# One transformer step on one core: FFN gate and up projections of ten blocks by Strassen's seven quarter products, hidden values through DRAM, down projection with the inner tiles outermost

## The reference, cut to what matters

```
h2 = _rmsnorm(x, norm2_g) * (1 + scale2) + shift2
a, b = jnp.split(h2 @ w_gu, 2, axis=-1)        # 1024 x 5632: gate half, up half
x = x + gate2 * ((jax.nn.silu(a) * b) @ w_down)   # 2816 x 1024
```

## Time and profile before

| what | us |
|---|---|
| median of 3 runs | 2062.1 (2058.85 to 2065.07) |
| the profiled execution, its time | 2066.32 |
| its span, first to last instruction | 2064.4 |
| PE busy | 1999.6 (97%) |
| DVE, ACT, POOL busy | 941.5, 609.5, 559.3 |

### The profile page before, as it was taken

The page is one execution under the profiler, slowest core; times in us unless marked ns, Lnnn a source line. Parts: engine busy times, 40 slices in busy tenths (PEclk is TensorE's granted clock), DMA queues, the critical chain, the costliest instruction groups (busy, mean ns, idle before and its releaser), DMA issues.

```text
span 2064.4 us, 26414 instructions
## 1 busy us (share of the span) xinstructions
PE 1999.6 (97%) x10768; PEld 1756.4 (85%) x10768; DVE 941.5 (46%) x1712; ACT 609.5 (30%) x1093; POOL 559.3 (27%) x392
## 2 busy tenths in 40 slices
PE   8999898899999999899999999999999999999998
PEld 3899788798889889788888888888888888888887
DVE  5699954255566665337416651312303213123035
ACT  3512222355455555344313211111111111111113
POOL 0000000434344442134432332232222222322225
PEclk9899999999999999999999999999999999999999
DMA  8552333733333441556520321111111111111112
GB/s 306 184 159 62 113 120 105 166 100 85 94 94 93 105 102 58 166 162 193 183 73 21 92 62 41 42 41 41 32 41 41 41 31 42 41 33 40 41 41 102
DMA packets 198807, 185.19 MB, mean 90 GB/s; under 512 B 33696, under 2 KB 174240, under 8 KB 197664
## 3 DMA queue, kind: packets, MB, share of 16 engines
q1 hardware_dynamic: 198688, 183.52, 29.7%
HBM read 142.60 MB, written 40.89 MB: 89 GB/s over the span
## 4 chain that ended last, share of the span: by engine, by line
PE 54%; DVE 2%; DMA 1%; issue 0%; ACT 0%; POOL 0%; SPq 0%; DVEq 0%; ACTq 0%
PE ps_all L144 53%; DMA branch_and_gates<-branch_dram 1%; DVE normed L2021 1%; DVE AL L2027 1%; DVE normed L2015 1%; DMA gates<-last_gates 0%; PE ps_all L1685 0%; DVE y L2063 0%; POOL w_lo L1904 0%; PE ps_all L1619 0%; PE ps_all L1618 0%; PE ps_all L1672 0%; DVE XT L1992 0%; PE ps_all L1643 0%; ACT w_hi L1762 0%
## 5 line engine op out<-in xcount | busy, mean ns | idle before, releaser
L144 PE MATMUL ps_all<-AH,w_hi 128*128 128x512 f32 (+3 forms) x2112 | 767.8, 364 | 31.7 <-PEq L229 7.4
L144 PE MATMUL ps_all<-AL,w_hi 128*128 128x512 f32 (+3 forms) x2112 | 756.2, 358 | 0.0
L144 PE MATMUL ps_all<-AH,w_lo 128*128 128x512 f32 (+3 forms) x2112 | 755.7, 358 | 0.0
L144 PEld LDWEIGHTS ps_all<-AH,w_hi 128*128 128x128 f32 x2112 | 403.8, 191 | 74.7 <-issue 23.2
L144 PEld LDWEIGHTS ps_all<-AH,w_lo 128*128 128x128 f32 x2112 | 402.8, 191 | 42.0
L144 PEld LDWEIGHTS ps_all<-AL,w_hi 128*128 128x128 f32 x2112 | 404.4, 191 | 39.1
L1904 POOL TENSOR_TENSOR w_lo<-w_raw,w_hi 128x1024 fp32r<-128x1024 f32 x78 | 194.6, 2494 | 555.7 <-ACT w_hi L1762 555.7
L1992 DVE SCALAR_TENSOR_TENSOR XT<-ps_all,mod,XT 128x512 f32<-128x512 f32 (+1 forms) x288 | 187.3, 662 | 204.3 <-PE ps_all L144 194.3
L2043 DVE TENSOR_TENSOR hidden<-ps_all,silu_a 128x512 f32<-128x512 f32 (+1 forms) x66 | 39.8, 602 | 504.1 <-PE ps_all L144 504.1
L144 PE MATMUL ps_all<-actH,w_hi 128*128 128x512 f32 (+1 forms) x528 | 188.7, 357 | 0.0
L144 PE MATMUL ps_all<-actL,w_hi 128*128 128x512 f32 (+1 forms) x528 | 188.3, 357 | 0.0
(11 more groups left out here) (172 smaller groups left out, 2538.2 us busy)
## 6 DMA issues: line engine op xcount, KB each, us to landing
w_raw<-w_gu_dram SPq DMA_DIRECT2D x44, 512.0 KB
w_raw<-w_in_dram SPq DMA_DIRECT2D x42, 512.0 KB
wmod_then_mixers<-w_mod_dram SPq DMA_DIRECT2D x20, 1024.0 KB, 8.8
branch_and_gates<-gates SPq DMA_DIRECT2D x16, 768.0 KB, 4.4
w_raw<-w_down_dram SPq DMA_DIRECT2D x22, 512.0 KB
gates<-gate_rows SPq DMA_DIRECT2D x42, 224.0 KB, 1.9
kq_src<-kT_dram SPq DMA_DIRECT2D x16, 384.0 KB, 6.0
xT_dram<-xT_then_mixers SPq DMA_DIRECT2D x1, 5120.0 KB, 17.3
```

The lines of the kernel that those rows point to most:

```text
L144: mm = nc.tensor.matmul(out, w, a[:, k, cols[0]:cols[1]], start=(first and part == 0), stop=(last and part == 2))
```

## The change

The first block (hidden tiles 0 and 1) is computed as before. For the other ten, each side (gate, up) of a block is one "pair" p, 20 in all: its 1024 x 256 weights are seen as 2 x 2 quarters (input half, hidden tile), the latent rows as 2 x 2 quarters (input half, chunk), and the product is made by Winograd's form of Strassen's method, with seven quarter products P1 to P7 of 4 input tiles x 3 matmuls x 512 columns instead of eight. The context chunk stays classic (X0, X1: 24 matmuls of 256 columns each).

- Row sums: `t_sums` makes four sums of row quarters once, 16 DVE instructions; ACT and DVE split them (`T_hi`, `T_lo`; one of them over the columns of chunk 1 in AH and AL).
- Weight sums: for each pair a 1 MB load (`load_pair`), 4 DVE instructions (`weight_sums`), and 8 slots of 128 x 512 (4 quarters, 4 sums), each split by ACT (`upper_slot`) and POOL (`lower_slot`). Ten slots form a ring.
- Results: for each pair ACT copies P1 and DVE makes 7 additions with one operand in PSUM (`add`); after the up side DVE multiplies the five quarters with the silu of the gate side (`hidden_quarter`).
- The hidden values go to DRAM by chunk and tile and come back in the down projection. That runs after all pairs, as 66 groups n = (chunk c, hidden tile k) with the chunk outermost: in each group 8 output tiles x 3 matmuls into 8 PSUM banks, summed over all k in PSUM (`down_group`). Each group loads a 512 KB row block of `w_down` (three raw buffers, four split ones) and its hidden chunk, so `w_down` is loaded and split three times.
- The residual rows are written back to DRAM before the normalisation, which now works in place, and are loaded again during the down projection; the output is added once, at the end of each chunk (`last_residual`).
- The final sums of squares and the transposes of chunks 0 and 1 run between the down groups of chunk 2. Four matmuls with zeros open the banks that two 256-column sums share.
- gate2 is made in 8 parts beside the first 8 pairs. After the first and the second phase POOL clears 59 and 31 semaphores.

```diff
...
+def clear(g):
+
+    for signal in g.used:
+        g.nc.gpsimd.sem_clear(signal)
...
+def product_order():
+
+    order = [(0, "P1")]
+    for p in range(PAIRS_FFN):
+        order += [(p, name) for name in (("P2", "P6", "X0") if p else ("P2", "X0", "P6")) + ("P5", "P7", "X1")]
+        order += [(p + 1, "P1")] if p + 1 < PAIRS_FFN else []
+        order += [(p, "P4"), (p, "P3")]
+    return order
...
+SUM_OF = {"u2": ("P6", "11", "12"), "11": ("P2", "11", "11"), "u3": ("P7", "12", "22"), "u4": ("P5", "12", "12"),
+          "21": ("P4", "22", "21"), "22": ("P5", "22", "22"), "12": ("P3", "12", "12")}
...
+                def load_down(n):
+                    if n == 0:
+                        sp.wait_ge(W.lo_ready, MIX + UNITS_DOWN)
+                        sp.wait_ge(acc_step, STEPS * KD)
+                    elif n < 3:
+                        sp.wait_ge(prod_done, PRODUCT_AT[LAST, "P2"] + 1)
+                    else:
+                        sp.wait_ge(W.lo_ready, MIX + UNITS_DOWN + n - 2)
+                    k = DOWN[n][1]
+                    sp.dma_start(down_raw(n), g.d["w_down"][k * P:(k + 1) * P, :].rearrange("p (j n) -> p j n", j=2)).then_inc(down_in[n % 3], 16)
...
+                def spill(c, first, last):
+                    a, b = RCH[c]
+                    sp.wait_ge(*released(("wo", last - 1, c)))
+                    sp.dma_start(g.d["xT"][first:last, :, a:b].rearrange("k p t -> p k t"), X[c][:, first:last, :]).then_inc(spilled[c], 16)
...
+                def load_pair(p):
+                    if p < 2:
+                        sp.wait_ge(t_lo, 12)
+                    else:
+                        sp.wait_ge(*lowered(8 * (p - 1) - 1))
+                    col = (p % 2) * HID + (p // 2 + 1) * 2 * P
+                    sp.dma_start(w_pair[p % 2][:, :, :], gu[:, :, col:col + 2 * P]).then_inc(pair_in[p % 2], 16)
...
+                operands = {"P1": (g.AH, g.AL, 0, 0), "P2": (g.AH, g.AL, 4, 0), "P6": (g.AH, g.AL, 0, WIDE), "P3": (g.AH, g.AL, 4, WIDE),
+                            "P5": (t_tiles(TH, 0), t_tiles(TL, 0), 0, 0), "P7": (t_tiles(TH, 1), t_tiles(TL, 1), 0, 0),
+                            "P4": (t_tiles(TH, 2), t_tiles(TL, 2), 0, 0)}
...
+                def quarter_product(p, name):
+                    out = g.ps_all[:, product_bank(p, name), :]
+                    pe.wait_ge(*lowered(8 * p + SLOTS_OF[name][-1]))
+                    if name != "X1":
+                        bank_wait(p, name)
+                    if p == 0 and name in ("P5", "P7", "P4"):
+                        pe.wait_ge(t_lo, 12)
+                    if (p, name) == (0, "P6"):
+                        pe.wait_ge(t2_lo, 4)
+                    if name[0] == "X":
+                        n = int(name[1])
+                        for half in range(2):
+                            hi, lo = slot(8 * p + SLOTS_OF[name][half])
+                            for k in range(4):
+                                w = slice(k * P, (k + 1) * P)
+                                mm = products(nc, out[:, n * CTX:(n + 1) * CTX], hi[:, w], lo[:, w], g.AH, g.AL, 4 * half + k, (LAT, T),
+                                              half == 0 and k == 0, half == 1 and k == 3)
+                    else:
+                        hi, lo = slot(8 * p + SLOTS_OF[name][0])
+                        ah, al, k0, a = operands[name]
+                        for k in range(4):
+                            w = slice(k * P, (k + 1) * P)
+                            mm = products(nc, out, hi[:, w], lo[:, w], ah, al, k0 + k, (a, a + WIDE), k == 0, k == 3)
+                    mm.then_inc(prod_done, 1)
+
...
+                def down_group(n):
+                    c, k = DOWN[n]
+                    hi, lo = down_weights(n)
+                    fetched(UNITS_DOWN + n)
+                    pe.wait_ge(hd_lo, n + 1)
+                    for m in range(KD):
+                        if k == 0:
+                            down_bank_wait(c, m)
+                        if c == 2 and k == 0 and m % 2 == 0:
+                            pe.wait_ge(zeros_ready, 1)
+                            nc.tensor.matmul(g.ps_all[:, m // 2, :], zeros[:, 0:P], zeros[:, :], start=True, stop=False)
+                        half, w = m // 4, slice(m % 4 * P, (m % 4 + 1) * P)
+                        mm = products(nc, down_bank(c, m), hi[:, half, w], lo[:, half, w], g.AH, g.AL, n % 4, (0, chunk(c)),
+                                      k == 0 and c < 2, k == HTILES - 1 and (c < 2 or m % 2 == 1))
+                        if k == HTILES - 1:
+                            mm.then_inc(m_done, 1)
+                    if k < HTILES - 1:
...
+                for p, name in PRODUCTS:
+                    quarter_product(p, name)
+                    if name == "P3" and p < KD:
+                        gate2_products(p)
+                for n in range(len(DOWN)):
+                    down_group(n)
+                    step = n - 2 * HTILES
+                    if step in (2, 11):
+                        final_stat(step // 11)
+                    if 3 <= step < 11 or 12 <= step < 20:
+                        y = step - 3 if step < 11 else step - 4
+                        turn(y // 2, y % 2)
                 final_stat(2)
...
+                def split_down(n):
+                    act.wait_ge(down_in[n % 3], 16 * (n // 3 + 1))
+                    if n >= 4:
+                        act.wait_ge(*group_done(n - 4))
+                    else:
+                        act.wait_ge(prod_done, PRODUCT_AT[LAST, ("P5", "P6", "P6", "P3")[n]] + 1)
+                    nc.scalar.activation(down_weights(n)[0], down_raw(n), ACT.Copy).then_inc(W.hi_ready, 1)
...
+                def upper_slot(n):
+                    p, idx = divmod(n, 8)
+                    if idx < 4:
+                        act.wait_ge(pair_in[p % 2], 16 * (p // 2 + 1))
+                    else:
+                        act.wait_ge(s_sum, 4 * p + SUM_STEP[idx])
+                    if n >= SLOT_RING:
+                        act.wait_ge(prod_done, slot_last_use(n - SLOT_RING) + 1)
+                    elif n >= 6:
+                        act.wait_ge(*finished(("b", 1, 2)))
+                    elif n >= 2:
+                        act.wait_ge(t2_lo, 4)
+                    else:
+                        act.wait_ge(t_lo, 12)
+                    nc.scalar.activation(tiles4(slot(n)[0]), in_pair(p, idx), ACT.Copy).then_inc(s_hi, 1)
...
+                def lower_slot(n):
+                    p, idx = divmod(n, 8)
+                    pool.wait_ge(s_hi, n + 1)
+                    hi, lo = slot(n)
+                    nc.gpsimd.tensor_tensor(tiles4(lo), in_pair(p, idx), tiles4(hi.bitcast(F32)), ALU.subtract).then_inc(s_lo, 1)
+
+                def lower_down(n):
+                    pool.wait_ge(W.hi_ready, MIX + UNITS_DOWN + n + 1)
+                    hi, lo = down_weights(n)
+                    nc.gpsimd.tensor_tensor(lo, down_raw(n), hi.bitcast(F32), ALU.subtract).then_inc(W.lo_ready, 1)
...
+                def t_sums(k):
+                    at = T_OPS * k
+                    nc.vector.tensor_tensor(X[0][:, k, :], X[1][:, k, :], X[0][:, k, :], ALU.subtract).then_inc(t_step, 1)
+                    dve.wait_ge(t_step, at + 1)
+                    nc.vector.tensor_tensor(X[1][:, k, :], X[1][:, 4 + k, :], X[1][:, k, :], ALU.subtract).then_inc(t_step, 1)
+                    nc.vector.tensor_tensor(T2[:, k, :], X[1][:, 4 + k, :], X[0][:, k, :], ALU.subtract).then_inc(t_step, 1)
+                    dve.wait_ge(t_step, at + 3)
+                    nc.vector.tensor_tensor(X[0][:, 4 + k, :], X[0][:, 4 + k, :], T2[:, k, :], ALU.subtract).then_inc(t_step, 1)
...
+                def weight_sums(p):
+                    a11, a12, a21, a22 = [in_pair(p, idx) for idx in range(4)]
+                    dve.wait_ge(*lowered(8 * p + 3))
+                    nc.vector.scalar_tensor_tensor(a22, a21, 1.0, a22, ALU.mult, ALU.add).then_inc(s_sum, 1)
+                    nc.vector.scalar_tensor_tensor(a21, a11, 1.0, a21, ALU.mult, ALU.subtract).then_inc(s_sum, 1)
+                    dve.wait_ge(s_sum, 4 * p + 2)
+                    nc.vector.scalar_tensor_tensor(a11, a22, 1.0, a11, ALU.mult, ALU.subtract).then_inc(s_sum, 1)
+                    dve.wait_ge(s_sum, 4 * p + 3)
+                    nc.vector.scalar_tensor_tensor(a12, a12, 1.0, a11, ALU.mult, ALU.subtract).then_inc(s_sum, 1)
...
+                for c in (0, 2):
+                    product(0, c)
+                t_sums(0)
+                t_sums(1)
+                t_lower(0)
+                product(0, 1)
+                t_sums(2)
+                t_lower(1)
+                t_sums(3)
+                t_lower(2)
+                t_lower(3)
+                product(1, 1)
+                for k in range(4):
+                    t2_lower(k)
+                for c in (0, 2):
+                    product(1, c)
+                weight_sums(0)
```

(28 more changed lines are left out.)

809 lines of the change are left out of this document (539 added, 270 removed).

## The result

The changed kernel takes 2017.57 us (median of four runs, 2016.56 to 2021.86), the kernel before 2062.35 (four runs, 2058.85 to 2065.07): ratio 0.9781, 95% interval 0.9766 to 0.9795. Forecast were 2013.5, with 2005 to 2034 as the range. The profiled execution of the changed kernel took 2021.86, with a span of 2020.0; the one before 2066.32, with 2064.4. So the two spans differ by 44.4, and all that follows accounts for that.

A forecast was written before the change was run, and what follows sets the result against it. PE, busy in 97% of the span, was taken to bound the kernel. Terms -54.3 - 1.7 + 0.9 + 1.9 + 2.1 + 1.5 + 1 + 0 = -48.6 from the 2062.1 median gave 2013.5 us, range 2005 to 2034.

The forecast's parts named there:

- step 8: Tail after the last down matmul: POOL's longer chain against transposes moved ahead and shorter sums, together 0, bounds -2 and +3.
- Step 1: Pairs: seven quarter products instead of eight, 240 fewer 512-column matmuls on PE, -54.3 us.
- Step 2: gate2 and zeros: 16 of 32 one-column matmuls left, -1.7 us; four matmuls with zeros, +0.9.
- Step 3: Pairs: POOL, ACT, DVE and loads keep PE fed through 24.8 us a pair, cost 0.
- Step 4: FFN start: DVE's two-operand instructions stretch POOL's weight lowering to 5.6 us, so PE waits, +1.9 us.
- Step 5: Hand-over from pairs to down projection: PE waits for DVE's sum, product and first hidden lower part, +2.1 us.
- Step 6: PE's clock falls after one of the two stalls, +1.5 us, bounds 0 and 3.
- Step 7: Down projection: same matmuls, but weights loaded and split for every group, +1 us, bounds 0 and 8.
- Step 9: Semaphore clears on POOL and the write-back of rows before the normalisation are hidden, costing nothing.
- starved down projection: Rival: POOL's lowering at 6.00 us starves the down projection, 87 us more, 2100, slower than before; chance 4%.
- pairs late by a microsecond each: Rival: an unseen wait in the ring of slots delays 20 pairs by 1 us each, +20, 2034; chance 7%.
- the matmul's distance: Rival: distance between matmuls grows to 0.24 from 0.226 us in 1680 of them, +23; chance 3%.

The follow-up runs named there:

- experiment 1: Changed kernel with the twelve matmuls of P3 issued twice in each pair, eight products instead of seven: 2072.12 us, ratio to before 1.0047.
- experiment 2: Changed kernel with POOL lowering every slot of the pairs twice in a row: 2097.52 us.
- experiment 6: Changed kernel with DVE's first three hidden lower parts put ahead of the last product's sum: 2016.74 us.
- experiment 4: Changed kernel with POOL lowering each chunk 2 down weight twice: 2047.28 us; S (time from the chain's first 25.01 row to the span's end) 832.0.
- experiment 9: Changed kernel loading 1024 columns of each hidden row in chunk 2 instead of the 256 used: 2019.41 us.
- experiment 7: Changed kernel with PE turning three of the last four halves ahead of the last token sums: 2015.11 us.
- experiment 8: Changed kernel without POOL's seven sums of chunk 2; ACT squares all eight tiles and PE adds them: 2012.73 us, ratio to before 0.9754.

## Why the prediction was right, point by point

The total was right, 4.1 us below the measured median, and nearly all of that is the tail. Up to the last down matmul the terms give -46.0 (-48.6, and the +2.6 that step 8 moves ahead of it), and -46.0 was measured; within that sum some terms erred against each other.

- **Step 1, the seven products: right.** -54.3 forecast; 54.6 when one product is put back (experiment 1).
- **Step 2: wrong by about 1.** I took half of the gate2 matmuls to go. The timeline shows x32 records in both kernels: 3.47 us before, eight times 0.34 now, -0.7 instead of -1.7. The four matmuls with zeros cost 0.24 each, as forecast.
- **Step 3, PE is fed in the pairs: right**, 24.8 us and no wait. The reason given, spare time on each engine, was not enough: experiment 2 has POOL at 83% of a pair and loses 80 us, since in every second of the first eight pairs DVE's gate2 steps wait for POOL's instructions one by one.
- **Step 4, the stall at the FFN's start: the wrong engine.** I took from the earlier trace rows that DVE's instructions stretch POOL's. At 1152.81 POOL kept its 2.42 and DVE waited, so w_lo was in time, and PE's 1.9 did not occur. The kernel before has that case too, in a gate2 series 12 us ahead of the one that I read, where a single step that takes 0.47 elsewhere took 2.62:

```profile
1160.09 2.45 POOL L1904 TENSOR_TENSOR w_lo<-w_raw,w_hi 128x1024 fp32r<-128x1024 f32 x1 [0.48 <-ACT w_hi L1762]
```
```profile
1160.21 2.62 DVE L2056 SCALAR_TENSOR_TENSOR gate_acc<-w_gate,silu_c,gate_acc 128x256 f32<-128x256 f32 x1
```

  The Trainium skill (SBUF — State Buffer, "Who interferes with whom") calls the port pair that the two engines share an exclusive lock and says that issue order decides who blocks; by it there was no stall or one of 4.3, and the trace agrees with the first. My row was no value in between either: in the earlier trace rows POOL's 5.60 ends at 1180.51, 2.3 behind the end of DVE's series (1172.62 + 5.62 = 1178.24), so it had waited out all of the series that was left. What did occur is a wait of 0.9 ahead of the pairs (0.9 to 1.7 in the profiles of kernels alike up to there), for DVE's product behind its lower parts, at the end of a chain of DVE, the pair's load (5.17 us) and ACT.
- **Step 5, the hand-over: right**, 2.30 against 2.1, and experiment 6 shows that it was DVE's order alone.
- **Step 6, the clock: right in this execution**, one fall, and by luck: of ten profiles with this wait four have it (last section). The timeline behind the hand-over has distances of 0.43 us from 1689.51 to 1692.50, the 1.2 GHz level; 241.22 against 239.64 in the kernels without it is 1.6, with 1.5 forecast.
- **Step 7, the down projection: +2.3 instead of +1, for another reason.** Neither loads nor POOL's time were short (experiments 4 and 9). In chunk 2 DVE had four lots of two additions beside halves and lower parts; one lot took 1.48 us, the three that met POOL's w_lo of 2.4 to 2.9 took 3.50 to 3.69; PE waited 0.87 and 1.5 for DVE. The step looked at what DVE does to POOL and not at the reverse.
- **Step 8, the tail: wrong, by 4 us.** I had 10.5 from the last down matmul to the end; it is 14.5. POOL's chain outlasts it by 5.1 and not 4; the token sums take 1.83 where they took 0.8 before, because PE has idled 5 us and its clock is down; the turns stand behind the sums at that clock and set the pace of the output halves; and the last store takes 3.3 rather than 2.7. Experiments 7 and 8 give 1.75 and 3.3 of it back. In my sum 4 was for POOL's chain, 2.6 for the halves, 2.7 for the store, which leaves 1.2 for sums and root; they took 5.1, 3.25, 3.3 and 2.9. The term was mis-sized in good part because I took PE's prices from a stage in which PE was busy.
- **Step 9: right**; DVE's normalisation starts at the same time within 0.04 us.

The rivals did not occur. The starved down projection is a real mechanism (26.8 us of S in experiment 4), with its threshold at an estimated 3.4 us a lowering; "pairs late by a microsecond each" is what experiment 2 provokes; the matmul's distance did not change. That the terms before the tail add up to exactly what was measured is luck to within 2 us: of the -51.55 of PE's busy time, -54.3, +4.0 for nine half turns now ahead of the last down matmul, +0.9 for zeros, +1.6 of the clock, -0.7 of gate2 and -1.6 of token sums with fewer matmuls make -50.1, and the last 1.4 I have not traced.

## What to carry to other kernels

Where one engine is busy without a gap, its saved instructions are worth their full distance, and the forecast is decided by the edges: the hand-overs between stages and the tail, where that engine idles and also runs at its lower clock. When work goes to DVE and POOL together, count which instructions meet and how long the single instruction is, since a short DVE instruction of two SBUF operands can wait out a whole POOL instruction that is under way; two halves on POOL instead of one instruction cost it 0.6 us and gave DVE back 1.1. Room for such an engine is to be tested with a doubled instruction rather than inferred from its share of busy time.

## What I had not expected of the hardware

- DVE waits for POOL one instruction at a time: fourteen steps of 0.27 us pitch (3.76 in all) took 15.24 beside POOL's row of 1.33 us instructions, while POOL was hardly slowed (8 in 10.68). In the kernel before it was POOL that waited out the rest of a series of 14 steps of DVE. The width of the steps, 256 columns there and 128 here, does not decide it: the kernel before has a 256-column step that waited 2.62 (step 4), and in experiment 2 a POOL instruction that began at 1290.70, within one of the series of 128-column steps that were not held up, took 1.77 instead of 1.3. What does decide it stays open.
- The same wait of PE at the hand-over, 2.3 to 2.4 us, was followed by a fall of the clock in four of ten profiles of kernels that have it (241.2 for the 1056 matmuls behind it) and by none in six (239.6). So a wait of this length costs 1.6 us more or nothing, and a forecast should carry it as a chance.
- DMA moved 335 GB/s for 30 us beside a PE that never waited.
